# The first output projection of a diffusion trunk: seven block products for eight

## The reference, cut to what matters

```
# layer 0, for latents and context, same weights
u, z = split(h @ w_in)                   # 1024 -> 2 x 2048
y    = real(fft2(u in 8 groups of 256))  # over tokens and features
x    = x + gate * ((y * silu(z)) @ w_out)   # w_out: 2048 -> 1024
# layer 1 starts with
h    = rmsnorm(x, norm_g[1]) * (1 + scale) + shift
q, k, v, z = split(h @ ret_w_in)
```

## Time and profile before

| | us |
|---|---|
| median of 3 runs | 943.7 (943.36 to 945.25) |
| the profiled execution | 944.72 |
| its span | 942.9 |
| TensorE busy | 923.8 |
| VectorE busy | 548.1 |
| ScalarE busy | 352.2 |
| GpSimd busy | 239.6 |
| granted TensorE clock, mean | 0.998 |

### The profile page before, as it was taken

How to read it: one execution, slowest core, us unless ns; L and a number is a source line. 1 busy time by engine, 2 the same in 40 slices (tenths; PEclk the granted TensorE clock), 3 DMA queues, 4 the chain that set the end, 5 groups by cost and what they waited for, 6 DMA issues and landing times.

```text
span 942.9 us, 13113 instructions
## 1 busy us (share of the span) xinstructions
PE 923.8 (98%) x4835; PEld 801.8 (85%) x4835; DVE 548.1 (58%) x804; ACT 352.2 (37%) x609; POOL 239.6 (25%) x243
## 2 busy tenths in 40 slices
PE   6999999999999999999999999999999999999996
PEld 5999998888888888888888888888888888888886
DVE  6898769999984422367444444435435445468333
ACT  8463343242232322354323334424323333354223
POOL 4259941755562000014100220012100221011001
PEclk9999999999999999999999999999999999999999
DMA  9752334555546211212211122202111121102222
GB/s 361 291 224 90 113 98 148 192 189 179 197 161 223 68 47 66 90 45 90 88 52 40 45 90 67 68 0 89 67 67 44 44 71 63 62 6 90 90 90 89
DMA packets 28747, 98.78 MB, mean 105 GB/s; under 512 B 3688, under 2 KB 5896, under 8 KB 28448
## 3 DMA queue, kind: packets, MB, share of 16 engines
q1 hardware_dynamic: 26688, 91.10, 28.2%
q0 software_dynamic: 1744, 6.84, 1.9%
q10 hardware_dynamic: 272, 0.26, 0.1%
HBM read 96.07 MB, written 2.10 MB: 104 GB/s over the span
## 4 chain that ended last, share of the span: by engine, by line
PE 91%; DMA 2%; ACT 2%; issue 2%; DVE 1%; POOL 1%; SPq 0%; POOLq 0%
PE banks L1749 30%; PE banks L1750 30%; PE banks L1751 29%; DMA raw<-stream 1%; DMA gate<-x_rows 1%; PE banks L1802 1%; ACT hreg L929 0%; POOL gate L663 0%; ACT dist L735 0%; DVE dist L1220 0%; PE banks L1876 0%; POOL gate L703 0%; PE banks L1894 0%; DVE wreg L1210 0%; POOL xreg L567 0%
## 5 line engine op out<-in xcount | busy, mean ns | idle before, releaser
L1749 PE MATMUL banks<-hreg,ring 128*128 128x512 f32 (+2 forms) x940 | 332.1, 353 | 0.9 <-DVE hreg L1358 0.4
L1750 PE MATMUL banks<-hreg,ring 128*128 128x512 f32 (+2 forms) x940 | 331.3, 352 | 0.0
L1751 PE MATMUL banks<-hreg,ring 128*128 128x512 f32 (+2 forms) x940 | 329.5, 351 | 0.0
L1120 DVE TENSOR_TENSOR ring<-raw,ring 128x512 fp32r<-128x512 f32 x192 | 142.2, 754 | 243.8 <-ACT ring L715 243.0
L715 ACT ACTIVATE ring<-raw 128x512 fp32r<-128x512 f32 x192 | 118.3, 629 | 363.2 <-PE banks L1751 287.6
L1749 PEld LDWEIGHTS banks<-hreg,ring 128*128 128x128 f32 x940 | 177.3, 189 | 25.5 <-issue 2.0
L1751 PEld LDWEIGHTS banks<-hreg,ring 128*128 128x128 f32 x940 | 176.8, 188 | 22.3
L1750 PEld LDWEIGHTS banks<-hreg,ring 128*128 128x128 f32 x940 | 177.4, 189 | 21.1 <-issue 0.2
L630 POOL TENSOR_TENSOR gate<-xreg,gate 128x257 f32<-128x257 f32 (+1 forms) x64 | 69.4, 1114 | 77.9 <-ACT gate L872 61.8
L1152 DVE CUSTOM_DVE_ANT_0 dist<-raw,gate 128x1024 bf16<-128x1024 f32 x64 | 83.4, 1303 | 3.8
L663 POOL TENSOR_TENSOR gate<-gate 128x512 f32<-128x512 f32 x12 | 17.1, 1429 | 250.7 <-ACT gate L953 249.9
(11 more groups left out here) (232 smaller groups left out, 1096.7 us busy)
## 6 DMA issues: line engine op xcount, KB each, us to landing
raw<-stream SPq DMA_DIRECT2D x148, 512.0 KB, 3.3
gate<-stream SPq DMA_DIRECT2D x10, 512.0 KB, 11.3
gate<-x_rows SPq DMA_DIRECT2D x6, 512.0 KB, 7.2
gate<-x_lat POOLq DMA_DIRECT2D x1, 2048.0 KB, 9.7
xreg<-x_lat POOLq DMA_DIRECT2D x1, 2048.0 KB, 11.3
out<-xreg SPq DMA_DIRECT2D x3, 384.0 KB, 2.6
xreg<-stream SPq DMA_DIRECT2D x2, 512.0 KB, 11.3
gate<-cond_in SPq DMA_DIRECT2D x2, 512.0 KB, 10.8
```

Of the source, the lines that this page charges most:

```text
L1120: dve.tensor_tensor(ring[:, n % 2, 1, c], raw[:, buf, c], f32(ring[:, n % 2, 0, c]), ALU.subtract).then_inc(split_done, 1)
L1749: pe.matmul(out, left[0], right[0], start=start, stop=False)
L1750: pe.matmul(out, left[0], right[1], start=False, stop=False)
L1751: return pe.matmul(out, left[1], right[0], start=False, stop=stop)
```

## The change: what it does

The projection is cut into 2 x 2 blocks in three ways: the output tiles in pairs (2i, 2i + 1), the contraction tiles in pairs (2k, 2k + 1), and the 768 columns in two halves of 384 (MIX). By Strassen's scheme the four blocks of an output pair come from 7 products instead of 8. `PRODUCTS` lists them: the weight blocks of each (one, or two that are added or, for product 4, subtracted) and to which output blocks it is added with which sign. `RIGHT` lists the sums or differences of right-hand blocks. A unit is one product for one output pair: 8 steps, 384 columns, one bank, 28 units in all (u = 4 * product + i). The first four units share their steps (`FIRST_ORDER`: for each, steps 0 to 5 of all four, then 6 and 7), so that the last groups may be split later.

- **Weights.** For products 0, 1, 5, 6 (`SUMMED`) the sum of two weight blocks is made in device memory: ScalarE's queue issues a copy of 2 MB (`sums` from `first_in`) in each of the u stage's groups 1 to 4, and GpSimd, ahead of each of gate groups 0 to 3, waits for the copy and adds 2 MB to it by an accumulating transfer (`add_weights`). Products 2 and 3 need no sum. For product 4 (`DIFFERENCE`, units 16 to 19) both blocks are loaded, half of each in one raw buffer, so that a unit takes two buffers; GpSimd subtracts in place (`subtract_weights`).
- **Right-hand sides.** Blocks (0,0) and (1,1) are split as they are; the other five (40 steps, `STEPS`) are formed by GpSimd (`sum_right`, two work buffers), copied high by ScalarE (`right_hi`), and made low by VectorE (`right_lo`), spread over units 3 to 18 by `UNIT_STEPS`. Products that come later take the homes of earlier ones (`HOMES`).
- **Gates.** Group 7 is gated by VectorE (`gate_last`) instead of GpSimd. The z of groups 6 and 7 is kept in `z_tmp`, in what was y of groups 0 to 3. Groups 4 and 5 are split inside the z stage. Every split is 384 wide, since only two of four blocks are split directly.
- **Evictions.** VectorE adds each product into one or two output blocks (`evict`), at the places given by `EVICT_AT`: up to four operations a unit.
- **Context keys.** The context's norm is taken during units 24 to 27 (`ctx_sum` inside unit 25), and the keys of the context for head 0 are projected right after unit 27 from two slots of their own ("kc"), 16 steps of 256 columns. The token sums and row spreads stand between these steps. Head 0 then projects its keys for the latents alone.

The core of the diff, by engine:

```
 @block.sync
+            for n, (u, second) in enumerate(RAW_USES):
+                buf, _ = MIX_FIRST[u, second]
+                if n < RAW_BUFS:
+                    sp.wait_ge(split_done, 2 * (SLOT_OUT0 - RAW_BUFS + n) + 2 + SPLIT0)
+                else:
+                    v, was_second = RAW_USES[n - RAW_BUFS]
+                    halves = 1 + was_second if v // 4 == DIFFERENCE else 2
+                    sp.wait_ge(split_done, 2 * (SLOT_OUT0 + v) + halves + SPLIT0)
+                if u // 4 in SUMMED:
+                    j = SUMMED.index(u // 4)
+                    sp.wait_ge(s_summed[j], 16)
+                    src = sums[4 * j + u % 4]
+                else:
+                    src = mix_in[PLAIN.index((u, second))]
+                sp.dma_start(raw[:, buf, :], src).then_inc(s_raw[buf], 16)
...
 @block.gpsimd
+            def add_weights(j):
+                pool.wait_ge(s_copied[j], 16)
+                pool.dma_start(sums[4 * j:4 * j + 4], second_in[4 * j:4 * j + 4],
+                               accum_op=ALU.add, max_dma_last_dim=8192).then_inc(s_summed[j], 16)
+            def subtract_weights(u):
+                if u // 4 == DIFFERENCE:
+                    for h in range(2):
+                        buf, landed = MIX_FIRST[u, h]
+                        pool.wait_ge(s_raw[buf], landed)
+                        pool.tensor_tensor(raw[:, buf, 0:SLOT // 2], raw[:, buf, 0:SLOT // 2],
+                                           raw[:, buf, SLOT // 2:], ALU.subtract).then_inc(mix_sum, 1)
+            def sum_right(n):
+                q, i = STEPS[n]
+                (r0, h0), (r1, h1), op = RIGHT[q]
+                if n >= 2:
+                    pool.wait_ge(blo, n - 1)
+                pool.tensor_tensor(right_sum[n % 2], gate0[:, 2 * i + r0, MIX * h0:MIX * h0 + MIX],
+                                   gate0[:, 2 * i + r1, MIX * h1:MIX * h1 + MIX], op).then_inc(bsum, 1)
+            for p in range(GROUPS - 2):
+                if p < len(SUMMED):
+                    add_weights(p)
                 gate_group(p)
...
+            pool.wait_ge(gated, 8 * (GROUPS - 1))
+            pool.wait_ge(gated_vec, 8)
             pool.dma_start(xl, x_lat).then_inc(s_xl2, 16)
             pool.dma_start(xc, x_ctx).then_inc(s_xc2, 16)
+            pool.wait_ge(s_row, 32 * GROUPS)
+            for u in range(UNITS):
+                subtract_weights(u + 1)
+                for n in UNIT_STEPS[u]:
+                    sum_right(n)
+                if u == 19:
+                    break
...
 @block.scalar
+                if 1 <= g <= len(SUMMED):
+                    act.dma_start(sums[4 * g - 4:4 * g], first_in[4 * g - 4:4 * g]).then_inc(s_copied[g - 1], 16)
+            def mix_hi(u):
+                for a in range(2):
+                    c = slice(a * SLOT // 2, (a + 1) * SLOT // 2)
+                    if u // 4 == DIFFERENCE:
+                        buf, _ = MIX_FIRST[u, a]
+                        src = raw[:, buf, 0:SLOT // 2]
+                        act.wait_ge(mix_sum, 2 * (u - 4 * DIFFERENCE) + a + 1)
+                    else:
+                        buf, landed = MIX_FIRST[u, 0]
+                        src = raw[:, buf, c]
+                        act.wait_ge(s_raw[buf], landed)
+                    act.wait_ge(slot_done, 2 * (RING_OUT0 + u) + (a + 1 - 4 + DONE0))
+                    act.activation(ring[:, u % 2, 0, c], src, ACT.Copy).then_inc(hi_done, 1)
+            for u in range(1, UNITS):
+                mix_hi(u)
+                if u in (1, 2):
+                    group_hi(GROUPS - 3 + u)
+                for n in UNIT_STEPS[u]:
+                    right_hi(n)
...
 @block.vector
+            gate_last(0)
+            for u in range(1, UNITS):
+                if u == 26:
+                    add_square(10)
+                    add_square(11)
+                mix_lo(u)
+                if u == 26:
+                    dve.wait_ge(root_done, 1)
+                    dve.reciprocal(rstd_t[:, LAT:TOK], rstd_t[:, LAT:TOK]).then_inc(rstd_done, 1)
+                if u == 27:
+                    add_square(12)
+                    for k in range(3):
+                        h1_low(k, 1, LAT, TOK)
+                if u == 1:
+                    gate_last(1)
+                    group_lo(GROUPS - 2)
+                if u == 2:
+                    group_lo(GROUPS - 1)
+                for n in UNIT_STEPS[u]:
+                    right_lo(n)
+                if u == 4:
...
+                    dve.wait_ge(s_xl2, 16)
+                    dve.wait_ge(s_xc2, 16)
+                for v in EVICT_AT.get(u, ()):
+                    evict(v)
...
+            lo("kc", 0, RING_KC)
+            add_square(13)
+            for k in range(3, KT):
+                h1_low(k, 1, LAT, TOK)
+            add_square(14)
+            evict(27)
+            lo("kc", 1, RING_KC + 1)
...
 @block.tensor
+            def unit(u):
+                q, i = divmod(u, 4)
+                if u >= 8:
+                    pe.wait_ge(mixed, mixed_by(u - 8))
...
+                    last = mm3(mix_bank(u), part_of(u % 2, P * k), (right(q, k, 0), right(q, k, 1)),
+                               k == 0, k == PAIRS - 1)
...
+                    if u == 25 and k == 4:
+                        ctx_sum()
```

The tables that set the order:

```
+STEPS = [(q, i) for q in (2, 3, 4, 6, 5) for i in range(PAIRS)]
+UNIT_STEPS = [[] for _ in range(UNITS)]
+for _n in range(len(STEPS)):
+    UNIT_STEPS[3 + 2 * (_n // 5) + (_n % 5) // 2 - (_n % 5 == 4)].append(_n)
+EVICT_AT = {5: (0, 1), 6: (2, 3, 4), 7: (5,), **{_u: (_u - 2,) for _u in range(8, 20)}, 20: (18, 19),
+            **{_u: (_u - 1,) for _u in range(21, UNITS)}}
```

More of the change, by code:

```diff
@@ L414, in _, with load @@
         def _(sp):
-            def load(phase, n, t):
+            def load(phase, n, t, skipped=0):
                 bufs = PHASES[phase][1]
@@ new lines, in group_hi, with right_hi @@
+            def group_hi(g):
+                for half in range(2):
+                    if g < GROUPS - 1:
+                        act.wait_ge(gated, 8 * g + 8)
+                    else:
+                        act.wait_ge(gated_vec, 4 * half + 4)
+                    act.activation(right(half, g, 0), gate0[:, 2 * g + half, MIX * half:MIX * half + MIX],
+                                   ACT.Copy).then_inc(ghi, 1)
+            def right_hi(n):
+                q, i = STEPS[n]
+                act.wait_ge(bsum, n + 1)
+                act.wait_ge(slot_done, 2 * (RING_OUT0 + {2: 0, 3: 0, 4: 4, 6: 8, 5: 12}[q]) + DONE0)
+                act.activation(right(q, i, 0), right_sum[n % 2], ACT.Copy).then_inc(bhi, 1)
@@ L992, in head @@
                 if first:
[L993 to L994 removed]
+                    act.wait_ge(slot_done, 2 * (RING_KC + 2) + DONE0)
+                    ctx_keys()
                     used(2)
@@ new lines, in group_lo, with right_lo @@
+            def group_lo(g):
+                for half in range(2):
+                    dve.wait_ge(ghi, 2 * g + half + 1)
+                    dve.tensor_tensor(right(half, g, 1), gate0[:, 2 * g + half, MIX * half:MIX * half + MIX],
+                                      f32(right(half, g, 0)), ALU.subtract).then_inc(glo, 1)
+            def right_lo(n):
+                q, i = STEPS[n]
+                dve.wait_ge(bhi, n + 1)
+                dve.tensor_tensor(right(q, i, 1), right_sum[n % 2], f32(right(q, i, 0)),
+                                  ALU.subtract).then_inc(blo, 1)
@@ new lines, in ctx_sum @@
+            def ctx_sum():
+                pe.wait_ge(mixed, mixed_by(23))
+                pe.wait_ge(acc_done, 2 * KT)
+                pe.matmul(bank(5, CTX), ones[:, :], acc_t[:, LAT:TOK], start=True,
+                          stop=True).then_inc(sum_sq_done, 1)
+            pe.wait_ge(z_done, 4 * GROUPS + 4)
+            for n, (i, k) in enumerate(FIRST_ORDER):
+                if n % 4 == 0:
+                    split(SLOT_OUT0 + n // 8, n // 4 % 2)
+                pe.wait_ge(glo, 2 * k + 1)
+                last = mm3(mix_bank(i), part_of(n // 8 % 2, P * (n % 8)), (right(0, k, 0), right(0, k, 1)),
+                           k == 0, k == PAIRS - 1)
+                if n % 4 == 3:
+                    last.then_inc(slot_done, 1)
@@ L1981, in token_sum @@
+            for u in range(4, UNITS):
+                unit(u)
             def token_sum(o, t, parts):
@@ L2217, in output @@
         return found
-    slots += output(fnet_out[order])
     quarter = QK // 4
     x1 = np.concatenate([np.arange(quarter), 2 * quarter + np.arange(quarter)])
+    first_halves = np.concatenate([x1, x1 + quarter])
+    slots += pairs(ret_in, all_rows, D + first_halves)
     for h in range(HEADS):
@@ L2231, in weight_stream @@
     slots += output(ret_out)
-    assert len(slots) == SLOTS
-    return np.stack(slots)
+    assert len(slots) == SLOTS - UNITS
+    return np.stack(slots), mixing(fnet_out[order])
 def columns(v):
```

525 lines of the change are left out of this document (291 added, 234 removed), and 7 rows, old and new, of the table PRODUCTS.

## The result

The changed kernel takes 1017.8 us (median; 1017.17 to 1018.48) against 943.5 of the kernel before in the same comparison: a ratio of 1.078 (95% interval 1.077 to 1.0795), slower by 74 us where 18.5 were forecast.

A forecast was written before the change was run, and what follows sets the result against it. The prediction took TensorE's chain of waits as the bound, columns alone in the projection. Terms -16.6 + 0.25 + 7.2 + 4.05 + 19.3 + 0.3 + 4.1 gave +18.6, so 962 us; range 950 to 974, 939 to 982 over all cases.

The forecast's parts named there:

- Columns: First output projection: fewer columns gain 16.1 us, an earlier start 0.5, in all -16.6.
- Rival 3: Projection: at 384 columns the weight load might set the pitch, gain only 7, time 971; chance 0.02.
- Transfers: Four copies in the u stage and four accumulations before gate groups 0 to 3: taken at 0, ends 0 and 10.
- Rival 2: z stage: new transfers crowd it, copies perhaps on four engines, some 23 us on top of the sum, 985; chance 0.15.
- Units 17 to 19: Product 4: serial turns of landing, subtraction, sum and splits take 11.0, 9.85, 11.15 us; +19.3, from 14 to 23.
- Units 5 to 7: Projection: VectorE waits for x loads, then has a backlog of evictions and sums; +7.2, or 3.6 if loads land by 295.
- Units 0 to 4: Projection's start: VectorE waits for the last edge rows before gating group 7, so slot 2 comes late; +0.25.
- Pace of units 8 to 16: Projection: VectorE needs 8.95 us a pair of units against 8.44, so slots come late; +4.05, ends 0 and 8.
- Rival 1: Units 5 to 16: VectorE keeps ahead, entering unit 16 with 5 us in hand; net -2.8, 941; chance 0.18.
- The end: Units 20 to 27 and after: 0.3 before the context sum, then key projection 0.9 and token sums 3.2 late, together 4.1.

The follow-up runs named there:

- e9: Changed kernel without transfers, one plain slot for product 4 without GpSimd's subtraction, early gate of group 6, right sums' low parts on ScalarE: 938.9 us, ratio 0.9953.
- e4: Changed kernel with product 4 loading one plain slot per unit and GpSimd's subtraction of weights gone, transfers kept: 993.3 us.
- k1: Kernel before the change, with TensorE held at three tile boundaries of its first output projection (3.0, 1.1 and 9.6 us of idling): 961.8 us.
- e7: Changed kernel without transfers, sums before subtractions (961.5 us), and last dots read elsewhere so GpSimd gates group 6 without waiting for them: 960.0 us.
- e1: Changed kernel without the four copies and the four accumulating transfers: 977.8 us.
- e5: Changed kernel, computing everything, with GpSimd's right-hand sums ahead of its weight subtractions in each unit: 1002.1 us.
- e8: Changed kernel without transfers, sums before subtractions (961.5 us), and the right sums' low parts written by ScalarE instead of VectorE: 946.1 us.
- e3: Changed kernel with GpSimd's four accumulating transfers replaced by plain copies of the same size, ScalarE's copies kept: 1007.2 us.
- c1: Changed kernel, computing everything, without device-memory copies: second block accumulated onto the raw slot two units ahead, GpSimd's sums before subtractions: 989.3 us.
- k2: c1 with plain transfers on GpSimd's queue in place of its 16 accumulations: 976.1 us.

## Why the prediction was wrong

- **Columns** (-16.6): right in mechanism; that the number is the same is luck. The passes, 0.173 each, gave back 16.6 for the 16.1 forecast, and e9 is faster than before; the other 0.5, from an earlier start, did not come. Rival 3 is out.
- **Transfers** ("I take 0; ends 0 and 10"): the step that failed. They cost 39.9. The sum of 49 us of all engines was there (by the queues it was some 66: 42 and 23), and so was the share of 0.5, but I spread the transfers over the stage and set VectorE's few us of cover against a load that is late on average. The row was also of the wrong stretch: from 163 to 180, where the first accumulation came to run, the kernel before already had 0.66. An accumulation comes in one piece: for its 15 to 17 us the share is 0.91 to 0.96, a slot due in 3.3 lands in 10 to 13, and the cover is 4.4.
- **Rival 2** named the right place, crowding in the z stage, but neither the size (985) nor the mechanism. A copy doesn't run on four engines: it landed in 8.7, where 2 MB from four engines would be 60 GB/s each and one has 21 by the 343 of all. In the trace a copy is 32 packets of 64 KB, of 2.9 us each, 94 us of packets in 8.7 us, so more than ten engines at once. The Trainium skill (DMA: Bandwidth & Descriptors, Why a DMA increments its semaphore by 16 and not by 1) has it that software can split a contiguous one-dimensional access pattern so that it is spread over up to 16 engines. The trace agrees with a spread; that it came about in this way it doesn't show.
- **Units 17 to 19** (+19.3): right in mechanism, the sum with some luck. Turns of 13.06, 10.54 and 11.12 for 11.0, 9.85, 11.15; gaps of 9.0, 4.9, 5.6 from start to start, together 19.1 over the usual step; e4 takes out 24.4 with the clock. The turns are 2.7 longer in all than forecast, but TensorE took 5.6 and 5.5 for units 17 and 18, not 4.22, at the lower clock, and that filled part of them.
- **The clock**: missing from the sum. I priced each gap at its length. Doubled steps added 13.2 in the projection and 22.0 in all, and k1 shows the cause. This is the second step that failed.
- **Units 5 to 7** (+7.2): the size holds in part, the reason doesn't. The x loads landed in 8.5 [for 11.3, rows 8] and nobody waited; only the backlog of evictions came, 3.9 at unit 7.
- **Units 0 to 4** (+0.25): missed. GpSimd's wait for the last dots is a new line of the diff; it started group 6 at 309.53, three us before the projection's first matmul, and slot 2 was 2.3 late. e7 says that it is worth 1.5 or less in the end. The 2.4 ahead of the first matmul belongs to the transfers: e1 doesn't have it.
- **Pace of units 8 to 16** (+4.05): 3.9 in the change. But e5 and e8 show more of it behind the turn: without transfers and in the better order it costs 15.4. Rival 1's lead for VectorE never existed: TensorE waited for its splits ahead of units 13 and 15.
- **The end** (+4.4): 3.4 before the token sums and 1.4 before the key projection as forecast, and 3.4 at units 24, 25 and the context sum, for 0.3.

With 40 for the transfers and 13 for the projection's clock, my +18.6 becomes +72; 73 was measured. That it closes so well is in part luck: units 5 to 7 cost 3.3 less than forecast and the end 3.8 more. No version that computes everything came under 943.5: even without the second blocks, in the better order, it is 961.5, and 15.4 of the 18 above the kernel before is VectorE's new work (e8).

## What to carry to other kernels

Price a new transfer in the stretch where it runs and not over the stage: if for its duration the engines are full, the loads beside it land about when it does, and only a buffer's worth of cover counts. Add to a long gap of TensorE the steps behind it: here 1.6 us behind a gap of 3.0 and 2.7 behind one of 9.6. When a serial turn is opened, look at once at the load of its busiest engine: the gain was 15.7 and not 25 because that stood next.

## What was not expected of the hardware

- Accumulating costs the DMA engines 1.7 times what a plain transfer of the same size does. GpSimd's queue took 6.0% of 16 engines' span of 1016.0 with four accumulations, 4.3% of 1004.8 with four plain transfers of the same size, 1.9% of 975.5 without: 42 us of all engines for 8 MB, against 25. By the packet it is twice: the median packet of 8 KB took 0.628 us with the addition and 0.309 without (the change, e3), one of 4 KB 0.328 and 0.159 (c1, k2). Into SBUF, 0.5 MB landed in 7.4 against 4.7.
- DMA engines can be at 0.96 of their time and move 238 to 255 GB/s.
- A row of 1.5 KB waits as long as a large slot beside such a transfer: 12.4 us. It was in the same queue as the transfer; the slots, in SyncE's queue, were as late.
- A gap of 3.0 us was enough to bring TensorE to its lower level (1.2 GHz) for 3.7 us.
